# A softplus series moved from VectorE to GpSimd, and a cumulation moved behind two products on TensorE

## The reference

```python
def _ssd_branch(z, xbc, dt_raw, conv_w, conv_b, dt_bias, a_log, d_skip, norm_w):
    xbc = silu(_centred_dwconv(xbc, conv_w, conv_b))          # 5 taps
    xs, bm, cm = split(xbc)                                   # x, B, C
    dt = softplus(dt_raw + dt_bias)                           # step sizes: 256 tokens x 2 directions x 32 heads
    a = -exp(a_log)
    y_fwd = _ssd_scan(xs * dt[0], dt[0] * a[0], bm, cm)
    y_bwd = flip(_ssd_scan(flip(xs * dt[1]), flip(dt[1] * a[1]), flip(bm), flip(cm)))
    ...

def _ssd_scan(xs, a, bm, cm):
    a_cum = cumsum(a)
    decay = exp(where(lower, a_cum[:, None] - a_cum[None, :], -inf))
    y_diag = einsum('bcqgn,bcsgn,bgrcqs,bcsgrp->bcqgrp', cm, bm, decay, xs)
    ...
```

## Time and profile before

| | us |
|---|---|
| median of 3 runs | 2491.35 (2488.61 to 2491.52) |
| the profiled execution's own time | 2490.21 |
| its span in the profile | 2488.4 |
| TensorE busy | 2418.7 (97%) |
| VectorE busy | 1717.0 (69%) |
| ScalarE busy | 1340.8 (54%) |
| GpSimd busy | 90.4 (4%) |

### The profile page before, as it was taken

How to read it: one execution, slowest core, us unless ns; L and a number is a source line. 1 busy time by engine, 2 the same in 40 slices (tenths; PEclk the granted TensorE clock), 3 DMA queues, 4 the chain that set the end, 5 groups by cost and what they waited for, 6 DMA issues and landing times.

```text
span 2488.4 us, 48741 instructions
## 1 busy us (share of the span) xinstructions
PE 2418.7 (97%) x18994; PEld 2314.9 (93%) x18994; DVE 1717.0 (69%) x2565; ACT 1340.8 (54%) x2355; POOL 90.4 (4%) x101
## 2 busy tenths in 40 slices
PE   8999999999999999999999999999999999999998
PEld 8898999999899999999999998799999999779998
DVE  7788676666888867676676576576657657668665
ACT  5788655543588855554454445554445444555443
POOL 0000000000100000000010010010001001001000
PEclk9999999999899999999999999999999999999999
DMA  7443444445444444444545545345554554534553
GB/s 214 135 153 119 153 150 139 153 135 181 124 136 143 129 153 142 147 151 137 186 152 169 174 147 140 95 134 186 177 175 154 169 174 147 139 108 142 192 181 112
DMA packets 397974, 376.07 MB, mean 151 GB/s; under 512 B 27199, under 2 KB 396013, under 8 KB 397693
## 3 DMA queue, kind: packets, MB, share of 16 engines
q1 hardware_dynamic: 397821, 373.94, 47.7%
HBM read 372.84 MB, written 1.05 MB: 150 GB/s over the span
## 4 chain that ended last, share of the span: by engine, by line
PE 76%; DVE 13%; ACT 4%; DVEq 2%; issue 1%; DMA 1%; SPq 1%; ACTq 0%
PE ps L582 21%; PE ps L584 21%; PE ps L583 21%; DVE scratch L1773 3%; DVE w_lo L1550 3%; DVEq L1772 1%; PE ps L803 1%; ACT w_hi L1080 1%; PE ps L834 1%; PE ps L835 1%; PE ps L836 1%; ACT scratch L1080 1%; DMA raw<-in_ffn_w_up 1%; ACT scratch L1077 1%; PE ps L857 1%
## 5 line engine op out<-in xcount | busy, mean ns | idle before, releaser
L1550 DVE TENSOR_TENSOR w_lo<-raw,w_hi 128x1024 fp32r<-128x1024 f32 x664 | 811.8, 1229 | 425.9 <-ACT w_hi L1080 425.6
L582 PE MATMUL ps<-x_hi,w_hi 128*128 128x256 f32 (+1 forms) x3664 | 1057.6, 289 | 16.2 <-DVE w_lo L1550 4.8
L583 PE MATMUL ps<-x_lo,w_hi 128*128 128x256 f32 (+1 forms) x3664 | 1043.9, 285 | 0.0
L584 PE MATMUL ps<-x_hi,w_lo 128*128 128x256 f32 (+1 forms) x3664 | 1040.5, 284 | 0.0
L1080 ACT ACTIVATE w_hi<-raw 128x1024 fp32r<-128x1024 f32 x664 | 694.7, 1055 | 453.9 <-PE ps L584 338.5
L582 PEld LDWEIGHTS ps<-x_hi,w_hi 128*128 128x128 f32 x3664 | 691.6, 189 | 43.1 <-issue 26.0
L583 PEld LDWEIGHTS ps<-x_lo,w_hi 128*128 128x128 f32 x3664 | 693.3, 189 | 2.2
L584 PEld LDWEIGHTS ps<-x_hi,w_lo 128*128 128x128 f32 x3664 | 694.9, 190 | 0.0
L582 PE MATMUL ps<-big_r,w_hi 128*128 128x272 f32 (+1 forms) x832 | 238.9, 287 | 0.0
L584 PE MATMUL ps<-big_r,w_lo 128*128 128x272 f32 (+1 forms) x832 | 238.1, 286 | 0.0
L1080 ACT ACTIVATE scratch<-ps 128x256 f32<-128x256 f32 (+9 forms) x328 | 122.8, 386 | 177.3 <-PE ps L836 77.5
(11 more groups left out here) (304 smaller groups left out, 3120.9 us busy)
## 6 DMA issues: line engine op xcount, KB each, us to landing
raw<-in_w_in SPq DMA_DIRECT2D x184, 512.0 KB, 4.8
raw<-in_ffn_w_up SPq DMA_DIRECT2D x176, 512.0 KB, 4.4
raw<-in_ffn_w_down SPq DMA_DIRECT2D x64, 512.0 KB, 4.3
raw<-in_mix_w_in SPq DMA_DIRECT2D x64, 512.0 KB, 4.6
scratch<-in_w_in SPq DMA_DIRECT2D x40, 512.0 KB, 4.8
raw<-in_w_mem_kv SPq DMA_DIRECT2D x32, 512.0 KB, 4.5
raw<-in_w_br_ssd SPq DMA_DIRECT2D x32, 512.0 KB, 4.2
raw<-in_ffn_w_down SPq DMA_DIRECT2D x32, 384.0 KB, 3.6
```

Source lines behind the costliest of these rows:

```text
L582: mm(out, wh, xh, start=first, stop=False)
L583: mm(out, wh, xl, start=False, stop=False)
L584: return mm(out, wl, xh, start=False, stop=last)
L1550: tt(w_lo[:, p % PARTS, :, :], raw_at(slot_of(Q, p))[:, :, (p % 2) * P:(p % 2 + 1) * P], wh_f[:, p % PARTS, :, :], ALU.subtract).then_inc( ...
```

## The change

The series goes to GpSimd: 9 `tensor_scalar` and 8 `tensor_tensor` of 128x128 with a drain ahead of each but the first. VectorE keeps what is ahead of it (up to s squared, which now releases GpSimd through `dt_squared`) and the max; what comes behind it (`dt_tok`, `a_tok`) becomes `dt_steps`, which waits for `dt_series` and stands behind `conv_silu(5)`. GpSimd's loop over the two layers is written out. On TensorE `cumulate` and the waits behind it move from ahead of the transposes to behind the product of C and B, and write banks 2 and 3 in place of 4 and 7.

```diff
@@ GpSimd
-            with pool.Fori(0, DEPTH) as l:
+            for l in range(DEPTH):
                 pool.drain()
                 pool.memset(cum_rows[2 * SSD_HEADS:P, :].bitcast(F32), 0.0).then_inc(S["rows_cleared"], 1)
                 pool.drain()
                 pool.memset(y_sum[:, :], 0.0)
+                s1, s2, series = dt_x[:, 4, :], dt_x[:, 5, :], dt_x[:, 6, :]
+                pool.drain()
+                pool.wait_ge(S["dt_squared"], l + 1)
+                pool.tensor_scalar(series, s2, 1.0 / 17, None, ALU.mult)
+                for c, x in ((15, s2), (13, s2), (11, s2), (9, s2), (7, s2), (5, s2), (3, s2), (1, s1)):
+                    pool.drain()
+                    pool.tensor_scalar(series, series, 1.0 / c, None, ALU.add)
+                    pool.drain()
+                    m = pool.tensor_tensor(series, series, x, ALU.mult)
+                m.then_inc(S["dt_series"], 1)
@@ TensorE, cumulate()
-                            mm(ps[4][:, t * 64 + d * SSD_HEADS:t * 64 + (d + 1) * SSD_HEADS], w, a_tok[:, src, c],
+                            mm(ps[2][:, t * 64 + d * SSD_HEADS:t * 64 + (d + 1) * SSD_HEADS], w, a_tok[:, src, c],
...
-                    rows_out = ps[7][0:SSD_HEADS, :]
+                    rows_out = ps[3][0:SSD_HEADS, :]
@@ TensorE, group
                     if l == g == 0:
                         pe.wait_ge(S["late_free"], 1)
-                    if g == 0:
-                        cumulate()
-                    if g == 0:
-                        pe.wait_ge(S["cum_ready"], l + 1)
-                        pe.wait_ge(S["row_ready"], l + 1)
-                        pe.wait_ge(S["rows_cleared"], l + 1)
                     pe.wait_ge(S["conv_ready"], G * 6 + 4)
...
                     m.then_inc(S["cb_done"], 1)
+                    if g == 0:
+                        cumulate()
+                        pe.wait_ge(S["cum_ready"], l + 1)
+                        pe.wait_ge(S["row_ready"], l + 1)
+                        pe.wait_ge(S["rows_cleared"], l + 1)
@@ ScalarE and VectorE read the rows from ps[3] and cum_tok from ps[2] (ps[7] and ps[4] before)
@@ VectorE, dt_softplus()
-                    tt(s2, s, s, ALU.mult)
-                    v.drain()
-                    ts(p_, s2, 1.0 / 17, None, ALU.mult)
-                    for c in (15, 13, 11, 9, 7, 5, 3):
-                        v.drain()
-                        stt(p_, p_, 1.0 / c, s2, ALU.add, ALU.mult)
-                    v.drain()
-                    stt(p_, p_, 1.0, s, ALU.add, ALU.mult)
+                    tt(s2, s, s, ALU.mult).then_inc(S["dt_squared"], 1)
                     ts(dt_x[:, 7, :], dt_x[:, 0, :], 0.0, None, ALU.max)
-                    v.drain()
+
+                def dt_steps():
+                    nega_l = flat(neg_a[:, ds(l, 1), :])
+                    p_ = dt_x[:, 6, :]
+                    v.wait_ge(S["dt_series"], l + 1)
                     stt(flat(dt_tok[:, :, :]), p_, 2.0, dt_x[:, 7, :], ALU.mult, ALU.add)
@@ VectorE, group
                     split(Q, 10)
                     conv_silu(5)
+                    if g == 0:
+                        dt_steps()
                     split(Q, 11)
                     split(Q, 12)
```

More of the change, by code:

```diff
@@ L344, in build @@
         params_in = sem("params_in")
-        names = ("idle_ready skip_ready mem_turned mem_ready x_turned xT_ready rows_turned rows_free late_turned late_free dt_hi_ready dt_lo_ready x_hi_ready mem_hi_ready rope_ready x_ready dt_done dt_pre dt_exp a_ready row_done row_hi row_ready cum_ready sel_ready rows_cleared first_tap conv_acc "
+        names = ("idle_ready skip_ready mem_turned mem_ready x_turned xT_ready rows_turned rows_free late_turned late_free dt_hi_ready dt_lo_ready x_hi_ready mem_hi_ready rope_ready x_ready dt_done dt_pre dt_exp dt_squared dt_series a_ready row_done row_hi row_ready cum_ready sel_ready rows_cleared first_tap conv_acc "
                  "conv_tanh conv_ready xs_turned xdt_ready cb_done bc_done expo_ready decay_ready w_ready y_done "
@@ L1243, in _ @@
                         act.wait_ge(S["row_done"], l + 1)
-                        copy(cum_rows[0:SSD_HEADS, :], ps[7][0:SSD_HEADS, :]).then_inc(S["row_hi"], 1)
-                        copy(cum_tok[:, :, :].rearrange("p t h -> p (t h)"), ps[4][:, 0:2 * 64]).then_inc(S["cum_ready"], 1)
+                        copy(cum_rows[0:SSD_HEADS, :], ps[3][0:SSD_HEADS, :]).then_inc(S["row_hi"], 1)
+                        copy(cum_tok[:, :, :].rearrange("p t h -> p (t h)"), ps[2][:, 0:2 * 64]).then_inc(S["cum_ready"], 1)
                         act.drain()
@@ L1733, in dt_softplus @@
                 def dt_softplus():
-                    nega_l = flat(neg_a[:, ds(l, 1), :])
                     if l == 0:
@@ L1738, in dt_softplus @@
                     v.wait_ge(S["dt_exp"], l + 1)
-                    u, s, s2, p_ = dt_x[:, 2, :], dt_x[:, 4, :], dt_x[:, 5, :], dt_x[:, 6, :]
+                    u, s, s2 = dt_x[:, 2, :], dt_x[:, 4, :], dt_x[:, 5, :]
                     ts(dt_x[:, 3, :], u, 2.0, None, ALU.add)
@@ L1799, in _ @@
                         v.wait_ge(S["row_hi"], l + 1)
-                        tt(cum_rows[SSD_HEADS:2 * SSD_HEADS, :], ps[7][0:SSD_HEADS, :], cum_rows[0:SSD_HEADS, :].bitcast(F32),
+                        tt(cum_rows[SSD_HEADS:2 * SSD_HEADS, :], ps[3][0:SSD_HEADS, :], cum_rows[0:SSD_HEADS, :].bitcast(F32),
                            ALU.subtract).then_inc(S["row_ready"], 1)
```

## The result

The changed kernel takes 2496.30 us (median of 11 runs, 2495.06 to 2497.35) where the kernel before, on the same chip, takes 2491.35 (11 runs, 2488.29 to 2493.93): a ratio of 1.0022, with a 95% interval of 1.0012 to 1.0031. It is slower by 5 us; I had forecast 2491.0, no change, with a range up to 2496.5. That range just holds the time, but only because it took in the time of rival 3; the forecast's own range ended at 2494.5. The profiled execution has a span of 2493.8 us.

The account below looks back on a forecast made before the run. TensorE, busy 97%, bounds the kernel, so only its waits and lower clock can win. On 2490.2 us, -3.1 for an earlier tile 9 and +4 for the clock gave 2491.1; own range 2487 to 2494.5, with rivals 2480 to 2496.5.

Parts of the forecast that it names:

- rival 3: Series on GpSimd slow at every turn, 14.8 us; `a_tok` at 62.3 and 678.4; 2497 us with the clock; chance 0.12.
- Step 1: Series leaves VectorE: its next pieces come 4.05 us sooner, both gaps before tile 8 and its lower clock go.
- Step 2: TensorE, behind tile 8: transposes and C times B run first, 1.6 to 1.9 us no longer behind the cumulation.
- Step 3: Series on GpSimd: 8.5 us alone, 11.8 us with turns against VectorE; `a_tok` at 59.2 and 675.3.
- Step 4: From `a_tok` to tile 9: 4.28 plus 0.64 us, tile 9 sooner by 1.3 and 1.8 us, sum 3.1.
- Step 5: TensorE's thin stretch behind tile 8: clock falls in both layers, 2 us a layer, handing back the gain.
- Rival 2: Series late, but TensorE's clock holds: 3.1 us won, 2487.1 us; chance 0.25.
- rival 1: Series on GpSimd in time, ending by 55.3: 9.1 us won, 2481.1 us; chance 0.15.

Follow-up runs that it names:

- kernel with products in the waits: Changed kernel plus 18 TensorE products nobody reads ahead of C times B and 14 ahead of the cumulation; 2494.76 us, run again 2492.70.
- the short series: Changed kernel with series terms 1/15 to 1/7 left out, 7 GpSimd instructions in place of 17; 2485.44 us, ratio 0.998 to the kernel before.
- the early rows: Against the kernel before: series one place later on VectorE, cumulation between transposes and C times B, rows copied and subtracted at once; 2481.19 us, ratio 0.9959.

## Why the prediction was wrong

Its mechanism was right in each part, and the order of its steps can be read in the profile. Two terms of the sum were mis-sized, and both to the same side.

- **Step 1 held in part.** Tile 8's gap went from 4.32 and 3.71 to 1.34 and 1.39 us, where I had said under 0.7. The clock was 1.00 in it. In layer 0 VectorE's square came 0.8 us later than in the profile before (47.16 against 46.36); VectorE is that much behind already at 26 us, long ahead of the series, so this is not the change's. The taps, split and SiLU that GpSimd delayed made up the rest.
- **Step 2** came in the order forecast, C times B at 58.1 instead of 56.6 to 57.
- **Step 3, the price of the series, failed.** I had taken 11.8 us and measured 12.8 and 13.0. The parts were off by more, in opposite directions. I had a one-input instruction at 0.30 us, from clearings that read nothing; it takes 0.53 (0.84 for the first). A drain takes 0.15 to 0.16, not 0.13. The two-input ones are 0.46, as worked out. That makes 11.2 us alone, not 8.5. Against it I had 3.3 us for the turns with VectorE, and it was 1.6, since the one-input half of the instructions never takes a turn. Two layers: 2.2 us too low. `a_tok` released TensorE at 61.17, behind the 60.5 from which I had called it rival 3, though 0.8 of this is the later square; in layer 1, from the square on, it came 14.2 us later where I had 12.9.
- **Step 4 held**: from the cumulation to the spread's start less what the clock costs is 6.91 - 2.63 = 4.28 us, as before, and nothing of VectorE's was late behind it.
- **Step 5, the price of the lower clock, failed, and by most.** I had it fall, as it did, but put it on tile 9, with a share of 0 to 1 us for the cumulation and no reason for so small a one. The cumulation from its start to its last row takes 5.47 us instead of 2.84: 2.63 us a layer, in both. In layer 1 the spread and tile 9 pay as well (0.35, and 689.97 - 686.15 = 3.82 instead of 2.85). Together 2.63 + 3.95 = 6.6 us, where I had 4.

Put right, the sum is 2491.1 + 2.2 + 2.6 = 2495.9 us, beside 2496.3 and 2494.8 measured. That it comes so close is partly luck: two things that it leaves out run against each other. The square of layer 0 was 0.8 us late from the start, and of the 3.2 us that tile 9 is late in layer 0 only 1.6 are left at the square of layer 1 (664.09 against 662.45). At 508.40 to 511.50 and at 648.30 to 650.60 us the profile before has a granted clock of 0.50 where the one after has 1.00.

Step 5 failed on the short products of 32 columns: they pay for the clock in full. The twelve go from 1.42 to 2.77 us, a factor of 1.95, more than a tile's 128x256 products, which start every 0.12 us at the higher clock and every 0.21 at the lower. The kernel with products in the waits confirms the price at its place, 6.5 us in the two layers.

Rival 2, the clock that holds, was wrong, and rival 1 was wrong from step 3 on: at 0.53 us an addition even the undisturbed series would end behind the last SiLU. Rival 3 had the right sign for half a right reason: `tensor_scalar` costs more than the addition, but not every instruction takes a turn.

## What to carry to other kernels

A move to an idle engine has to be priced as latency on the way to its reader, not as busy time: GpSimd was busy for 4% of the span, and took 12.8 us for what VectorE does in 3.2. Where a chain is short and TensorE waits for it, move less urgent pieces behind it on the fast engine and look at who reads each result next; here that gave -8.4 us where the engine change gave +5. Nearly all of that came only when the copy and the subtraction of the rows moved too. Where TensorE will wait, price what stands behind the wait at the lower clock, short products above all. Check gains at the end of the program: one transfer 1.6 ms later, 2.6 us longer in landing, took back a good part of one here. And before comparing two profiles look where each profiled execution stands among its kernel's runs.

## What the runs showed of the hardware

- On GpSimd a one-input `tensor_scalar` of 128x128 float32 takes 0.53 us and is the dearer one: a `tensor_tensor` takes 0.46 undisturbed. VectorE takes 0.22 and 0.29 for them. The Trainium skill, GPSIMD Engine Reference, § 4.1 (Engine selection) has it the other way round, a factor of about 2 for two inputs and "1-input is roughly line-rate"; here it is 1.6 for two inputs and 2.4 for one, so the measurement decides.
- Only GpSimd's two-input instructions wait for VectorE. All 16 additions took 0.53 us, beside splits and taps too, while the 16 products had a mean of 0.69 and took 1.0 or 1.46 where they began beside a split. VectorE pays in turn: beside a product a SiLU takes 0.67 instead of 0.42 and a tap 0.66 to 0.78 instead of 0.48. The one-input instructions cost it less: the five splits that began 0.04 to 0.05 us behind the start of an addition took 1.32 us, the one that began with GpSimd idle 1.22. The same reference, § 1 (Specifications), names contention for VectorE's side of it (two SBUF inputs), and the trace agrees with that; that one-input instructions of GpSimd do not wait is seen only in these rows.
- The lower clock can follow short waits: in the short series a wait of 1.56 us had 0.50 behind it. It need not: behind the 1.66 and 2.08 us of the early rows it stayed at 1.00, and so it did where idle products filled the waits.
